# Reordering the first loads, the first attention scores, a retention norm's squares and one weight split in a two-block diffusion transformer

## The reference

```python
def modulate(t, gain, shift, scale):
    return rmsnorm(t, gain) * (1 + scale) + shift
...
qkv = jax.nn.silu(conv_fn(p_qkv, conv_w))          # block 1: first use of h @ w_in
...
for layer in range(DEPTH_2):                       # block 2, two layers
    mod = (silu_c @ ada_w[layer] + ada_b[layer])[:, None, :]
    ...
    h = _rmsnorm(x, norm_w[layer, 0]) * (1.0 + sc1) + sh1
    y, yc = _ret_mlstm_mixer(...)   or   y, yc = _window_attn_mixer(...)
    x = x + g1 * y
    x = x + g2 * _swiglu(_rmsnorm(x, norm_w[layer, 1]) * (1.0 + sc2) + sh2, ffn_w_in[layer], ffn_w_out[layer])
...
r = _rmsnorm(jnp.transpose(r, (0, 2, 1, 3)), ret_norm_w.reshape(H_RET, HEAD_DIM))   # retention's norm
s_win = jnp.einsum('bnqhgd,bnkhd->bnhgqk', qb, kw).astype(f32) * scale              # attention scores
```

## Time and profile before

| | |
|---|---|
| median of 3 runs | 1800.56 us (1798.06 to 1804.52) |
| profiled execution, its own time | 1803.1 us |
| its span, first to last instruction | 1801.3 us |
| mean granted TensorE clock | 0.98 |
| PE busy | 1707.7 us, 95% |
| DVE, ACT, POOL busy | 52%, 41%, 33% |
| HBM read | 259.44 MB, 145 GB/s over the span |

### The profile page before, as it was taken

The page is one execution under the profiler, slowest core; times in us unless marked ns, Lnnn a source line. Parts: engine busy times, 40 slices in busy tenths (PEclk is TensorE's granted clock), DMA queues, the critical chain, the costliest instruction groups (busy, mean ns, idle before and its releaser), DMA issues.

```text
span 1801.3 us, 33659 instructions
## 1 busy us (share of the span) xinstructions
PE 1707.7 (95%) x14306; PEld 1495.9 (83%) x14306; DVE 932.1 (52%) x1722; ACT 734.4 (41%) x1273; POOL 591.3 (33%) x302
## 2 busy tenths in 40 slices
PE   4999998989999999999999889999999989999998
PEld 1888997878889999697798667888888777689998
DVE  1757126666453333544487736565455456744333
ACT  2564522232455465431555334212212345754443
POOL 0246222121134443124233124454445311134443
PEclk7999999999999999999999999999999989999999
DMA  8534334332455454423220233334556322035453
GB/s 322 197 133 149 117 141 175 149 149 92 178 211 199 176 182 164 159 75 141 82 94 25 81 143 117 140 140 152 187 206 238 141 82 95 1 130 178 185 188 117
DMA packets 37876, 262.66 MB, mean 146 GB/s; under 512 B 4192, under 2 KB 4320, under 8 KB 8416
## 3 DMA queue, kind: packets, MB, share of 16 engines
q1 hardware_dynamic: 37728, 260.51, 39.2%
HBM read 259.44 MB, written 1.05 MB: 145 GB/s over the span
## 4 chain that ended last, share of the span: by engine, by line
PE 83%; DVE 7%; DMA 3%; ACT 3%; issue 2%; POOL 2%; SPq 0%; DVEq 0%; ACTq 0%; POOLq 0%
PE ps L957 20%; PE ps L959 19%; PE ps L958 19%; PE ps L986 2%; PE ps L1011 2%; DMA raw<-in_mod 2%; POOL wl L825 1%; PE ps L975 1%; PE ps L977 1%; PE ps L976 1%; PE ps L1319 1%; PE ps L1035 1%; PE ps L1665 1%; PE ps L1687 1%; ACT wh L1717 1%
## 5 line engine op out<-in xcount | busy, mean ns | idle before, releaser
L825 POOL TENSOR_TENSOR wl<-raw,wh 128x1024 fp32r<-128x1024 f32 (+1 forms) x213 | 518.6, 2437 | 957.8 <-ACT wh L1717 957.8
L957 PE MATMUL ps<-h_hi,wh 128*128 128x256 f32 (+1 forms) x1696 | 547.2, 323 | 7.8 <-POOL wl L825 6.1
L958 PE MATMUL ps<-h_lo,wh 128*128 128x256 f32 (+1 forms) x1696 | 542.0, 320 | 0.0
L959 PE MATMUL ps<-h_hi,wl 128*128 128x256 f32 (+1 forms) x1696 | 542.0, 320 | 0.0
L1717 ACT ACTIVATE wh<-raw 128x1024 fp32r<-128x1024 f32 (+1 forms) x330 | 341.6, 1040 | 382.9 <-PE ps L959 229.3
L957 PEld LDWEIGHTS ps<-h_hi,wh 128*128 128x128 f32 x1696 | 323.7, 191 | 35.9 <-POOL wl L825 8.2
L958 PEld LDWEIGHTS ps<-h_lo,wh 128*128 128x128 f32 x1696 | 323.9, 191 | 22.7
L959 PEld LDWEIGHTS ps<-h_hi,wl 128*128 128x128 f32 x1696 | 323.7, 191 | 22.7
L2266 DVE TENSOR_TENSOR wl<-raw,wh 128x1024 fp32r<-128x1024 f32 (+1 forms) x117 | 147.3, 1259 | 208.7 <-ACT wh L1717 208.5
L957 PE MATMUL ps<-gh,wh 128*128 128x256 f32 (+1 forms) x528 | 169.3, 321 | 0.2 <-POOL wl L825 0.2
L958 PE MATMUL ps<-gl,wh 128*128 128x256 f32 (+1 forms) x528 | 168.1, 318 | 0.0
(11 more groups left out here) (447 smaller groups left out, 2544.6 us busy)
## 6 DMA issues: line engine op xcount, KB each, us to landing
raw<-in_ffn_in SPq DMA_DIRECT2D x66, 1024.0 KB, 4.8
raw<-in_mod SPq DMA_DIRECT2D x48, 1024.0 KB, 6.3
raw<-in_ffn_out SPq DMA_DIRECT2D x24, 1024.0 KB, 4.8
raw<-in_w_in SPq DMA_DIRECT2D x16, 1024.0 KB, 4.8
raw<-in_rlat SPq DMA_DIRECT2D x16, 1024.0 KB, 4.9
raw<-in_w_gate SPq DMA_DIRECT2D x12, 1024.0 KB, 4.8
raw<-in_w_ab SPq DMA_DIRECT2D x12, 1024.0 KB, 4.9
raw<-in_ffn_out SPq DMA_DIRECT2D x12, 768.0 KB, 4.3
```

What stands on the lines that cost most here:

```text
L825: nc.gpsimd.tensor_tensor(wl[e % SPLIT][:, 0:entries[e]["words"]], part(e), wh[e % SPLIT][:, 0:entries[e]["words"]].bitcast(F32), ALU.subt ...
L957: nc.tensor.matmul(b[:, cols], wh[e % SPLIT][:, w], xh(k), start=(k == 0), stop=False)
L958: nc.tensor.matmul(b[:, cols], wh[e % SPLIT][:, w], xl(k), start=False, stop=False)
L959: ins = nc.tensor.matmul(b[:, cols], wl[e % SPLIT][:, w], xh(k), start=False, stop=(k == nk - 1))
```

## The change

Five edits are made.

1. **First chunks.** The first `w_in` chunk is loaded ahead of everything but the small constants, and ACT, POOL and DVE split it before the inputs are normed. The eight first conditioning chunks come in another order: the four of the scale (4 to 7), then the shift's 0 and 1, then 2 and 3. One group of chunk products precedes the norm on PE (`mod_one(amid)`). The shift's second half is read in the midst of the first pair of dense tiles (`last_shifts`, at k = 2 and 3), and DVE's `first_norm` scales all tiles without waiting for shifts; tiles 4 to 7 lie in `sil` for that.
2. **Root's table** of a1 is loaded before the last square (`call_root`).
3. **Retention.** The first two squares stand at m = 3 of the loop, not m = 4.
4. **Scores.** Unit 0's scores are made before `query_sums` 6 and 7, and DVE masks them before rotating tiles 6 and 7.
5. **Third weight part.** `ahead("fa1", 0)` and `ahead("fa2", 0)` stand right behind the root (ACT) and the reciprocal (DVE) of b2 and c2, ahead of the scaling and shifting; `BEHIND_NORM` gives these two entries to DVE.

```diff
+BEHIND_NORM = (("fa1", 1), ("fa2", 1))
@@ entry
         by = 1 if keys[0][0] in ALL_POOL + SWIGLU_2 else len(entries) % 2
+        if keys[0] in BEHIND_NORM:
+            by = 0
@@ make_plan
-    norm("a1")
-    mod(4)
-    mod(4)
+    load("w_in", 0, [("qkv", 0), ("qkv", 1)])
+    mods[0] = 4
+    mod(4, ("ss", "a1"))
     spread("a1")
     mod(0)
-    for j in range(6):
+    mods[0] = 0
+    mod(2)
+    mod(0)
+    mod(2)
+    mod(0)
+    mods[0] = MODS_FIRST
+    use([("qkv", 0), ("qkv", 1)])
+    mod(2)
+    for j in range(1, 6):
@@ SyncE
-        sp.dma_start(res_c[:], dram["ctx"]).then_inc(sem("x_in"), 16)
-        sp.dma_start(res_l[:], dram["x"]).then_inc(sem("x_in"), 16)
...
+            if n == 0:
+                sp.dma_start(res_c[:], dram["ctx"]).then_inc(sem("x_in"), 16)
+                sp.dma_start(res_l[:], dram["x"]).then_inc(sem("x_in"), 16)
@@ TensorE
-        norm("a1")
-        mod(2)
+        mod_one(lambda: norm("a1"))
         spread("a1")
-        mod()
-
-        hdense_pair([("qkv", 0), ("qkv", 1)], "a1")
+        mod(3)
+
+        def last_shifts(k):
+
+            if k in (2, 3):
+                mod()
+
+        hdense_pair([("qkv", 0), ("qkv", 1)], "a1", last_shifts)
@@ TensorE, attention
+        query_scores(0)
         for i in (6, 7):
             query_sums(i)
@@ ScalarE
+                if (name, k) == ("a1", KD - 1):
+                    call_root()
...
+                if name == "a1" and k % 4 == 0:
+                    mod(2)
+                    evacuated(act, "modcol", 1 + k // 4)
...
+        ahead("qkv", 0, depth=2)
         act.wait_ge(sem("x_in"), 32)
         norm("a1", (CT, LT))
-        mod(3)
-        ahead("qkv", 0, depth=2)
+        mod()
         shift("a1", 0, (CT, LT))
+        mod()
...
-            if m == 4:
+            if m == 3:
                 evacuated(act, "RB", 3)
                 evacuated(act, "RO", 3)
-                head_norm(rout, "rsq", "rss", (0, 1))
+                for i in range(2):
+                    A(msq[:, i, :], rout[:, i, :], ACT.Square).then_inc(sem("rsq"), 1)
+            if m == 4:
+                full(act, "rss", 0)
+                free(A(hrc[:, 0, :], bank("rss", 0)[:, 0:P], ACT.Sqrt, bias=eps), "rss", 0)
...
         root("b2")
+        ahead("fa1", 0)
...
         root("c2")
+        ahead("fa2", 0)
@@ VectorE
+        def first_norm():
...
+            full(dve, "sp", "a1")
+            for k in range(5):
+                scaled(k)
+            mod(2)
+            scaled(5)
+            for k in range(4):
+                shifted_lo(k)
+            scaled(6)
+            scaled(7)
+            free(V.memset(rdone[:], 0.0), "sp", "a1")
+            mod(2)
+            for k in range(4, KD):
+                shifted_lo(k)
...
+        ahead("qkv", 0, depth=2)
         dve.wait_ge(sem("x_in"), 32)
         inverse("a1")
-        mod(3)
-        ahead("qkv", 0, depth=2)
-        norm("a1", 0, (CT, LT))
+        mod(2)
+        first_norm()
...
         inverse("b2")
+        ahead("fa1", 0)
         norm("b2", 3, (CT, LT))
...
+            if i == 6:
+                dve.wait_ge(sem("window_in"), 16)
+                masked(0)
...
         inverse("c2")
+        ahead("fa2", 0)
         norm("c2", 5, (LT,))
```

More of the change, by code:

```diff
@@ L165, in make_plan, with mod @@
     mods, mod_calls, early_read = [0], [], [0]
-    def mod(count):
+    def mod(count, amid=None):
         g = sum(c > 0 for _, c, _ in mod_calls)
@@ L176, in mod @@
                 chunks[-1]["read"] = early_read[0]
+        if amid:
+            add(*amid)
+            for n in range(mods[0], mods[0] + count):
+                chunks[n - mods[0] - count]["last"] = len(tile)
         if count:
@@ L1015, in mod_one @@
                         ins.then_inc(sem("mod_read"), 1)
+                    if a == 0 and amid:
+                        amid()
+                        begin("modrow", g)
                 close(ins)
@@ L1647, in query_sums, with query_scores @@
             close(nc.tensor.matmul(begin("aqsw", i)[:, 0:L], K2("swap"), aq[:, i, :], start=True, stop=True))
+        def query_scores(w_):
+            i, qt = w_ // 2, w_ % 2
+            if w_ in (0, 8):
+                evacuated(pe, "aksp", i // 4)
+            pe.wait_ge(sem("aq_ready"), i + 1)
+            b = [begin("as", w_, hf) for hf in range(2)]
+            for hf, h in enumerate(HALF):
+                close(nc.tensor.matmul(b[hf], aq[h, i, P * qt:P * qt + P], ak[h, i // 4, :], start=True, stop=True))
         for i in range(8):
@@ L1679, in _ @@
                 close(ins)
[L1680 to L1688, removed]
+            if 0 < u + 1 < 16:
+                query_scores(u + 1)
             if 1 <= u <= 16:
@@ L1768, in shift @@
                     v = 0 if r is res_l else 1
-                    ins = A(h_hi[:, k, cc], hraw[:, k % 4, cc], ACT.Identity,
+                    ins = A(h_hi[:, k, cc], unshifted(name, k)[:, cc], ACT.Identity,
                             bias=mods[:, lay, 8 * sec + k, v:v + 1])
@@ L2360, in _, with scaled, shifted_lo @@
         CT, LT = (res_c, slice(0, L)), (res_l, slice(L, T))
+        def first_norm():
+            both = ((res_c, slice(0, L), 1), (res_l, slice(L, T), 0))
+            def scaled(k):
+                for r, cc, v in both:
+                    ins = V.scalar_tensor_tensor(unshifted("a1", k)[:, cc], r[:, k, :], coef[:, 0, k, v:v + 1],
+                                                 bank("sp", "a1")[:, cc], ALU.mult, ALU.mult)
+                ins.then_inc(sem("a1_mul"), 1)
+            def shifted_lo(k):
+                dve.wait_ge(sem("a1_hi"), k + 1)
+                for r, cc, v in both:
+                    ins = V.scalar_tensor_tensor(h_lo[:, k, cc], unshifted("a1", k)[:, cc], mods[:, 0, k, v:v + 1],
+                                                 h_hi[:, k, cc].bitcast(F32), ALU.add, ALU.subtract)
+                ins.then_inc(sem("a1_h"), 1)
+            full(dve, "sp", "a1")
[11 more added lines that the diff above has]
+                shifted_lo(k)
         def ffn(nm, lay, halves, early=None):
```

59 lines of the change are left out of this document (34 added, 25 removed).

## The result

The changed kernel took **1789.4 us** (median of 4, 1787.81 to 1791.63) against 1801.93 us for the kernel before in the same session (median of 4, 1798.06 to 1804.52): ratio 0.9933, 95% interval 0.9916 to 0.9951, 12.5 us faster. The profiled execution took 1787.81 us, its span is 1786.0 us (before 1801.3), its mean granted clock 0.988.

What follows compares the result with a forecast made beforehand. The first stretch was taken as bound by transfers, then an ACT, PE and DVE chain, with PE busy 95% of the span. Terms -7.3 -3.5 -2.1 -1.0 +0.5 = -13.4 us from 1800.56 gave 1787.2 us; range 1783 to 1795.

Steps and rivals of the forecast that it cites:

- Front, -7.3: First stretch: first dense matmul at 35.2 instead of 45.09, first pair's end at 51.6 instead of 58.91; bounds -9 to -4.
- tile 4: Inside the first pair: products of chunks 2 and 3 end at 42.6, h_hi of this tile comes at 46.0.
- The landing times: First stretch: inputs land at 14.2, chunk 4 at 16.6, chunk 7 at 24, chunk 0 at 27.4, chunk 1 at 30 to 31.2.
- The rule against the first edit: First pair: the skill says short matmul bursts between transfer waits start cold again; by it the sum would be rival B's.
- the row: Earlier profile's clock windows: after a wait the uninterrupted first pair ran at 0.51 for 6 us, then at 1.00.
- rival B: First pair wholly at 1.2 GHz, ending at 60.1; sum -4.9 us, time 1795.7 us; chance 0.09.
- C: First chunks: transfer bubbles grow, chunks 1 to 3 land 2 us later; front -2.5, sum -8.6, 1792.0 us; chance 0.14.
- D: First stretch: the weights' split holds SP and 1.2 GHz outlasts the pair; slower, 1808.2 us with 25 us beyond; chance 0.02.
- Retention, -3.5: Retention's squares: the 1.81 us wait goes and 1.7 us of lower clock behind it; bounds -1.8 and -3.6.
- Scores, -2.1: First attention unit: PE goes on at 1513.95 instead of 1516.06, a 1.8 us wait remains, no clock gain counted.
- The cap of 2.8: Scores: no more than 2.8 us can come, since unit 1's exponentials end at 1517.66 as before.
- Third part, -1.0 and +0.5: Third weight part: b2 loses PE's 1.08 us wait for POOL's remainder (-0.5 to -1.5); c2's pair starts 0.5 us later.

Runs made afterwards that it cites:

- weights_first: The kernel before with only the first weights loaded ahead of the inputs and split early, conditioning chunks in their old order: 1802.76 us, ratio 1.0006.
- before_again: The kernel before, unchanged, executed once more for a second trace: span 1799.0 us.
- front_only: The changed kernel with the retention, scores and third weight part edits undone, leaving the first chunks' edit and the root's table: 1793.82 us, ratio 0.9958.
- no_table: The changed kernel without the early load of the root's table ahead of a1's last square: 1786.51 us, ratio 0.9919.

## Why the prediction was right, step by step

The forecast was -13.4 us. The times gave -12.5 and -9.2; the account gives -8.3 -1.9 -3.2 -0.1 = -13.5 (the front by the pair's mean end, the others by the rows of the edits). That is agreement in the sum by luck: retention was put 1.6 us too high and the third part 0.4, the front 1.0 too low and the scores 1.1, and these cancel.

**Front, -7.3: right in mechanism, 1 us too small.** In the seven traces with the front as changed the first dense matmul stands at 33.68 to 36.66 (mean 34.9, predicted 35.2), and the pair ends at 49.97 to 52.56 (mean 50.9, predicted 51.6); before's two traces end at 58.91 and 59.44. -8.3 in the mean, inside the bounds of -4 to -9. The missing 1 us is three small ones: the products of chunks 2 and 3 inside the pair took 1.87 us (39.06 to 40.93) instead of 2.3, the first dense matmul stands 0.3 us sooner in the mean, and before's own pair ends 0.3 us later in the mean of its two traces than in the one that I had. What was said of tile 4 held: ACT began its h_hi at 43.34, and PE took it at 44.30, 3.4 us behind the products' end, as forecast (42.6 to 46.0). The landing times held within 0.4 us in the first trace, but chunk 1 came anywhere from 28.97 to 31.95 in the seven.

**The rule against the first edit.** The Trainium skill, "TensorE: Matmul & The Clock Gate", section "HAM oscillation — how this bites in real kernels", has bursts start cold after a wait for a transfer. The traces agree with the row, not with rival B: chunks 2 and 3 interrupt the pair with work, not with a wait, and the granted clock stays at 1.00. No run here puts a wait for a transfer into the pair, so what it would cost isn't shown. Whether the pair is whole or not matters little (0.7 us in the mean). Rivals B, C and D are out in all seven traces: no pair ended after 52.6.

**Retention, -3.5: half of it wrong.** The step that failed is "which costs 0.39 times 4.4, 1.7 us", counted as an effect of the wait. Of five traces with the wait of 1.81 us two have the low clock behind it (the first of before, weights_first) and three don't. The edit gives the wait, 1.9 us, in every trace. The clock is no fixed price of the wait: at most it comes back in some executions, since none of the nine traces without the wait has a low clock there. Two of five against none of nine is too little to tell whether the wait brings it. The lower bound, -1.8, was the right value for the other three.

**Scores, -2.1: too small.** The wait came out as forecast (1.68, predicted 1.8), ACT's table and two exponentials set it, and a new wait of 0.74 us took some back: 1.45 us net. The step that failed is "the wait left is 1.8 us, as long as retention's that lowered the clock, so I count no clock back". The four traces of before's order in the table all have the low clock behind 3.87 us (windows at 0.50 and 0.67), the eight traces with 1.68 us none; that is the other 1.7 us of 3.2. The cap of 2.8 held as far as unit 1, which PE took 2.9 us sooner against the start of the stretch; it left out that unit 1's transposes then run at the high clock, 1.09 us instead of 1.77.

**Third part, -1.0 and +0.5: both too large.** In b2 DVE was not late: scaling starts 1.20 us behind the spread with the edit and without. In c2 it was, and the pair started 0.45 us later. The step that failed in b2 is "In b2 PE waits 1.08 us for POOL's remainder", taken as what every execution pays. The wait is 1.08 us in the first trace of before, whose pair has little low clock; in before_again and front_only, with more, POOL's remainder is in time, in weights_first 0.54 us is left, and the edit gave 0.3 to 0.4 us where it was traced. In c2 PE makes up most of the late start in the pair, and 0.16 to 0.29 us is left at the end. The net is near nothing.

**Left open.** Why the low clock comes at 528, in retention, at 960 and at 1000 in some traces and not in others isn't settled; of before's order the first trace and weights_first share one pattern, before_again and most of the changed kernels another. The length of one wait doesn't decide it: at c2 all fourteen traces have a low stretch, behind waits of 1.2 to 1.7 us. Also open are whether a whole first pair is better by 0.7 us, and how the front's 7 us divide between the order of the chunks and DVE's.

## What to carry to other kernels

A drop of the granted clock seen once behind a wait is a sample, not a price: take a second trace before it enters a sum, or enter it as a bound. A wait and a stretch of low clock hide each other, so a wait on another engine's work is worth its length only in those executions in which PE has the high clock. When chunks feed both a long chain (scale, coefficient, scaling) and a short one (shift), load the long chain's first and work on it while the rest arrive. Whether that rest is then read ahead of the work behind it or in its midst made little difference here, and loading weights earlier alone bought nothing. When a sum of terms comes out right, check the terms: here four were off by 0.4 to 1.6 us and cancelled.

## What the runs showed of the hardware

- ACT's table load (1.28 us) ran ahead of the wait of the instruction that needs it: at 18.01 in no_table, with the sums not ready until 20.9. A hand-made early load is idle work where the engine would have stood waiting there anyway.
- The low clock behind a wait of 1.81 us came in two of five traces at one place; behind 1.68 us at another place in none of eight, behind 2.54 us there it came in the one trace (0.66 for 5 us), behind 3.87 us there in all five.
- A DVE addition on 128x16 values took 2.05 us instead of 0.17 to 0.18 when it began while POOL subtracted a weight part (39.38 to 41.72), and ended with it. It is no single case: in before_again it took 1.68 us (from 40.48, POOL to 42.13), and in the first trace the addition on 128x8 values at 1088.49 took 2.31 us, under POOL's subtraction from 1088.41 to 1090.78. Operations that read an input from PSUM were not held: the scaled sums into `res_l` took 0.48 us also where they began under POOL's subtraction (27 times). Nor was a reciprocal, 0.18 us at 1508.37. No run here takes POOL alone away, so the cause is read from these rows.
- The time at which PE can read a chunk varies by 3 us between executions in the program's first 32 us (chunk 1: 28.97 to 31.95), which alone is a quarter of what this change moved.
